# Softmax denominators in attention: a diagonal of reciprocal sums, as two fp32r parts and two wide matmuls

## The reference, cut to what matters

```
def one_block(qi):
    s = jnp.einsum('bhqd,bhkd->bhqk', qi, k).astype(jnp.float32) * scale
    p = jax.nn.softmax(s, axis=-1).astype(v.dtype)
    return jnp.einsum('bhqk,bhkd->bhqd', p, v)
...
yx = (ox * jax.nn.silu(gx)) @ mla_w_o[j]
```

## Time and profile before

| | |
|---|---|
| time, median of 3 runs | 3262.49 us (3260.82 to 3264.07) |
| the profiled execution | 3262.19 us, its span 3260.2 us |
| mean granted TensorE clock | 0.972 of full speed |
| busy over the span | PE 92%, PEld 77%, DVE 54%, ACT 44%, POOL 13% |
| denominator matmuls in the trace | from 682 to 2015 us |

### The profile page before, as it was taken

How to read it: one execution, slowest core, us unless ns; L and a number is a source line. 1 busy time by engine, 2 the same in 40 slices (tenths; PEclk the granted TensorE clock), 3 DMA queues, 4 the chain that set the end, 5 groups by cost and what they waited for, 6 DMA issues and landing times. The chain is left out here.

```text
span 3260.2 us, 44295 instructions
## 1 busy us (share of the span) xinstructions
PE 3001.7 (92%) x15091; PEld 2495.0 (77%) x15091; DVE 1757.5 (54%) x2927; ACT 1422.4 (44%) x2971; POOL 431.0 (13%) x285
## 2 busy tenths in 40 slices
PE   2999999699999999999999998996899999997798
PEld 2878878588888878787878886784688888886677
DVE  6654554366766666767676765435233323333554
ACT  3554545356555655555555554325111111112543
POOL 1000000010111111110111110003011111112331
PEclk9999999899999999999999999997899999998899
DMA  6546455511112121211111100533222222213443
GB/s 219 182 158 228 147 178 182 174 51 44 51 33 69 40 70 40 69 36 44 50 55 54 40 27 29 203 127 123 71 70 70 65 68 73 70 54 125 134 155 103
DMA packets 217944, 308.07 MB, mean 94 GB/s; under 512 B 81008, under 2 KB 142720, under 8 KB 216576
## 3 DMA queue, kind: packets, MB, share of 16 engines
q1 hardware_dynamic: 213120, 296.98, 28.0%
q10 hardware_dynamic: 4608, 8.39, 0.7%
HBM read 213.94 MB, written 91.37 MB: 94 GB/s over the span
## 5 line engine op out<-in xcount | busy, mean ns | idle before, releaser
L1086 ACT ACTIVATE at_prob<-at_S,at_nmax 128x512 f32<-128x512 f32 (+1 forms) x640 | 411.4, 659 | 371.6 <-DVE at_nmax L1200 367.8
L1223 DVE TENSOR_TENSOR at_ptlo<-at_T,at_pthi 128x512 fp32r<-128x512 f32 x576 | 396.7, 689 | 319.4 <-ACT at_pthi L1102 318.3
L1102 ACT ACTIVATE at_pthi<-at_T 128x512 fp32r<-128x512 f32 x576 | 349.2, 609 | 225.4 <-PE at_T L972 225.4
L1189 DVE TENSOR_REDUCE at_mx<-at_S 128x1 f32<-128x512 f32 (+1 forms) x640 | 393.6, 630 | 84.2 <-PE at_S L946 77.4
L972 PE MATMUL at_T<-ident,at_prob 128*128 128x128 f32 x2304 | 345.8, 272 | 3.2 <-DVE at_ptlo L1223 3.2
L972 PEld LDWEIGHTS at_T<-ident,at_prob 128*128 128x128 f32 x2304 | 278.3, 140 | 69.4 <-DVE at_ptlo L1223 16.6
L95 PE MATMUL ci_ps<-h1hi,ci_whi 128*128 128x512 f32 x768 | 300.1, 391 | 17.6 <-DVE ci_wlo L1651 17.6
L96 PE MATMUL ci_ps<-h1lo,ci_whi 128*128 128x512 f32 x768 | 299.8, 390 | 0.0
L97 PE MATMUL ci_ps<-h1hi,ci_wlo 128*128 128x512 f32 x768 | 299.7, 390 | 0.0
L941 PE MATMUL at_S<-at_khi,at_qhi 128*128 128x512 f32 (+1 forms) x640 | 249.7, 390 | 48.6 <-ACT at_prob L1086 25.8
L95 PE MATMUL at_O<-at_pthi,at_vhi 128*128 128x512 f32 x576 | 272.8, 474 | 0.6 <-DVE at_og L1232 0.5
(11 more groups left out here) (202 smaller groups left out, 6391.9 us busy)
## 6 DMA issues: line engine op xcount, KB each, us to landing
fr_w<-in_w_front SPq DMA_DIRECT2D x75, 512.0 KB, 4.1
at_wmod<-in_w_mod SPq DMA_DIRECT2D x32, 512.0 KB, 3.3
ci_w<-in_cv_w_in SPq DMA_DIRECT2D x24, 512.0 KB, 4.2
fr_w<-in_w_front SPq DMA_DIRECT2D x24, 384.0 KB, 3.9
values<-fr_ob SPq DMA_DIRECT2D x36, 256.0 KB, 2.9
at_kst<-k_nope SPq DMA_DIRECT2D x8, 1152.0 KB, 7.3
at_vst<-values SPq DMA_DIRECT2D x8, 1152.0 KB, 7.3
fr_x<-in_x SPq DMA_DIRECT2D x16, 512.0 KB, 6.6
```

What stands on the lines that cost most here:

```text
L1086: nc.scalar.activation(prob[:, j % 2, i, k], S[:, c, 0:k.stop - k.start], ACT.Exp, scale=SCALE, bias=nmax[:, i % 2:i % 2 + 1], accum_out=l ...
L1102: nc.scalar.activation(dst, T[:, (n + SLOTS * j) % 2], ACT.Copy).then_inc(s_hi, 1)
L1189: nc.vector.tensor_reduce(mx[:, i % 2, c:c + 1], S[:, c, 0:k.stop - k.start], AXX, ALU.max).then_inc(s_mx, 1)
L1223: nc.vector.tensor_tensor(ptlo[:, kt % 3], T[:, (n + SLOTS * j) % 2], pthi[:, kt % 3].bitcast(F32), ALU.subtract).then_inc(s_lo, 1)
```

## The change

The diagonal is written twice: `dghi` is the product rounded to fp32r by a TENSOR_SCALAR, `dglo` the product less `dghi`, by a SCALAR_TENSOR_TENSOR that waits for the first through a new semaphore. PE multiplies fp32r ones with each, 512 columns at once, and adds the two in PSUM. The ones are a new tile that DVE fills once ahead of attention.

```diff
-        dg = sb("dg", [P, 2, BLK])
+        dghi, dglo = sb("dghi", [P, 2, BLK], F32R), sb("dglo", [P, 2, BLK], F32R)
+        ones = sb("ones", [P, P], F32R)
...
                 if kt == "den":
                     pe.wait_ge(s_dg, b * QT + QT)
-                    for i in range(QT):
-                        mm = nc.tensor.matmul(out[:, i * P:(i + 1) * P], net.ones[:], dg[:, j % 2, i * P:(i + 1) * P],
-                                              start=True, stop=True)
+                    nc.tensor.matmul(out, ones[:], dghi[:, j % 2], start=True, stop=False)
+                    mm = nc.tensor.matmul(out, ones[:], dglo[:, j % 2], start=False, stop=True)
...
             pe.wait_ge(s_kr, 1)
+            pe.wait_ge(s_ones, 1)
...
                     dve.wait_ge(s_tr, (b - 1) * SLOTS)
-                nc.vector.tensor_scalar(dg[:, j % 2, i * P:(i + 1) * P], net.ident[:], rl[:, i % 2:i % 2 + 1], None,
-                                        ALU.mult).then_inc(s_dg, 1)
+                q = slice(i * P, (i + 1) * P)
+                nc.vector.tensor_scalar(dghi[:, j % 2, q], net.ident[:], rl[:, i % 2:i % 2 + 1], None,
+                                        ALU.mult).then_inc(s_dghi, 1)
+                dve.wait_ge(s_dghi, t + 1)
+                nc.vector.scalar_tensor_tensor(out=dglo[:, j % 2, q], in0=net.ident[:], scalar=rl[:, i % 2:i % 2 + 1],
+                                               in1=dghi[:, j % 2, q].bitcast(F32), op0=ALU.mult,
+                                               op1=ALU.subtract).then_inc(s_dg, 1)
...
+            nc.vector.memset(ones[:].bitcast(F32), 1.0).then_inc(s_ones, 1)
             dve.wait_ge(s_krhi, 1)
```

More of the change, by code:

```diff
@@ L838, in attention @@
         (s_k, s_v, s_krin, s_krhi, s_kr, s_khi, s_klo, s_vhi, s_vlo, s_qhi, s_qlo, s_qk, s_mx, s_nmax, s_exp, s_rl, s_dg,
-         s_tr, s_hi, s_lo, s_mm, s_gden, s_og, s_recip) = (net.sem("at_" + n) for n in (
+         s_tr, s_hi, s_lo, s_mm, s_gden, s_og, s_recip, s_dghi, s_ones) = (net.sem("at_" + n) for n in (
              "k_in", "v_in", "kr_in", "krhi", "kr", "khi", "klo", "vhi", "vlo", "qhi", "qlo", "qk", "mx", "nmax", "exp",
-             "rl", "dg", "tr", "hi", "lo", "mm", "gden", "og", "recip"))
+             "rl", "dg", "tr", "hi", "lo", "mm", "gden", "og", "recip", "dghi", "ones"))
         VC = 3
```

## The result

The changed kernel takes 3308.82 us in the median (3305.6 to 3311.86, 4 runs). The kernel before, on the same chip, takes 3261.79 us (3260.82 to 3264.07). The ratio is 1.014, with an interval from 1.0125 to 1.0154. That is slower, by 47 us where 36 were forecast, and 0.8 us above the upper end of the range.

The account below looks back on a forecast made before the run. PE was taken as the bound, 1282.97 of 1300 us busy. DVE's delays sum to 4.92 us a loop head, 29.5 over six, plus 3.9 (head 0) and 2.6 (head 7): +36.0 on 3262.2, 3298 us; range 3268 to 3308.

Parts of the forecast that it names:

- PE's gain: Slot 9 on PE: three matmuls of 0.23 us in place of 1.12 us, 0.42 us a block, lost whole.
- Step 2: Step 2 of every phase: DVE's second product waits behind GpSimd, next maximum 0.88 us later, 0.60 in phase j = 3.
- second rival: Slower by DVE's plain time alone, the new product not losing to GpSimd: +11 us, 3273 us; chance 0.18.
- bare steps: Steps where DVE runs without a pause to `at_nmax` and PE already waits: they pay 0.39, 0.39 and 0.37 us.
- the loop's turn: Where engines jump back to the loop's first instruction: half of step 3 of j = 3's cost carried through, 0.20 us.
- last reserve: Beyond the counted terms, a delayed GpSimd chain or the whole 0.39 us through the turn could add 10 us.

Follow-up runs that it names:

- PE's part alone: The changed kernel without DVE's second product, `dglo` filled with zeros once, against the kernel before: 3262.39 us, ratio 0.9993.
- padded change: The changed kernel with eight fills of one unread column each in DVE's program ahead of attention: 3307.32 us, ratio 1.0136 to the kernel before.
- two padded kernels: Unread one-column fills on DVE ahead of attention: eight added to the changed kernel, 3307.32 us; 20 added to the kernel before, 3270.73 us.
- held run: The changed kernel with GpSimd's modulation held until DVE is through step 2's maxima: 3274.16 us, ratio 1.0038 to the kernel before.

## Why the prediction was right, and where it was off

- **PE's gain.** It is 0.23 us for each of the three matmuls, as said, and lost whole, as said. PE's part alone showed the loss (0.9993), and the two kernels with the products between the last two `low` showed that the gain is real (41.98 against 42.40 us).
- **Step 2.** The dependent product loses the race to GpSimd. The forecast delay was 0.88 us, with 0.73 of GpSimd in it; the trace has 0.89. In 31 of the 32 blocks the product is held. Holding GpSimd back took away 35 us where the forecast had 25 between its time and the second rival's; that run frees more than the new product, as said above.
- **The bare steps.** They pay 0.39 us where DVE runs without a pause. The intervals to j = 1 and to j = 3 have these terms in them and are right within 0.09 us.
- **What was off: the loop's turn.** The sum has for it "What step 3 of j = 3 pays may be carried through the loop's turn; I count half of it, 0.20". The interval over the turn was forecast to grow by 1.19 us and grew by 3.5 on the mean of five (17.7 us). That is 11.7 us more than counted. Added to the 36 it gives 48; measured are 47. The term itself was about right: in the padded change the two turns with neither a second pause nor a fall of the clock took 46.94 and 47.13 us, 1.1 to 1.2 more than the same turns before (45.86 and 45.96). Two terms were not in the sum at all. One is the second pause, about 1.5 us a turn, which the two padded kernels tie to the place of the code. The other is the granted clock, which fell at four of the five turns: 1.2 us where it can be read alone, 0.2 to 1.0 us at these turns, by their distance from the turn without a fall. That the longer waits of PE bring these falls about fits the rows and was not tested. Nor is the pause simply to be had back: with the 8 fills it was gone, and the time hardly moved.
- **The range.** The time is 0.8 us above its upper end. Taken by the ratio, from the 3262.2 us that the sum starts from, it is just inside: 1.014 x 3262.2 = 3307.9. Its last reserve, "a delayed GpSimd chain or the whole 0.39 through the turn could add 10 us", had the size of what was missing but neither cause in it, so that the time came out this close is luck.
- **The second rival** (DVE's plain time, 3273 us) failed as a forecast. The held run came out at 3274 us, but that is a coincidence. Away from the turns it lost only some 3 us, with part of PE's gain back (the interval to j = 2 is shorter than before), and the turns made up the rest.

The Trainium skill (SBUF — State Buffer, "SBUF: two separate sides") says that of a DVE instruction with two SBUF inputs and a GpSimd one, whichever starts first blocks the other to its end. The trace agrees for the new product: it has two SBUF inputs, and it waits out the GpSimd instruction that began before it, in the rows above by 0.04 us. The same skill (Runtime: NRT & Kernel Launch, "Instruction fetch mechanics") says that instructions come in blocks of 256, that crossing into the next block is mostly hidden, and that a taken branch whose target lies outside the two blocks at hand stalls. The trace agrees in so far as DVE has a pause at a turn (2.39 and 2.87 us). It does not agree that the crossing is mostly hidden, if the second pause, 1.48 us just behind the turn, is one. No run here shows the fetches themselves, so that cause was argued and not shown.

## What to carry to other kernels

When an engine at 99% waits only rarely, ask what those waits are for, and cost what a change adds on that chain, a dependent pair next to a chain on GpSimd by how the two interleave. Before giving such a change up, look for a place where nothing queues behind the added work: there the same split went from +1.4% to -0.6%. Allow some us for the turns of a hardware loop whose body grows, and look at the granted clock by stretches: a mean of 0.99 can hide falls to half speed just behind the waits that the change made longer.

## What the runs showed of the hardware

- Eight or twenty tiny instructions ahead of a loop switch a pause of 1.5 us on DVE at each turn off or on (1.50 and 1.48 us, ended by "issue" in these rows).
- In the changed kernel TensorE's granted clock fell to half of full speed (1.2 of 2.4 GHz) for 3.4 us at a time, four times, right behind waits of 2.11 to 2.23 us. One fall cost 1.2 us between two slots 9 of the padded change (45.93 against 44.7 us).
- A 128x128 product of DVE that waits for GpSimd took up to 0.85 us in place of 0.35 in the changed kernel and 1.26 in the run with the pair between the last two `low` and GpSimd held. In the first the chain behind it came 0.89 us later; the second is among the fastest kernels here.
- A 128x128 product of the identity with fp32r output takes DVE 0.29 us as TENSOR_SCALAR and 0.35 as SCALAR_TENSOR_TENSOR. Rounding to fp32r cost nothing: the fp32 one took 0.288.
- On PE an fp32r matmul of 512 columns takes 0.23 us. Four fp32 ones of 128 columns cost 0.81 and the matmul behind them 0.08 more.
